# Hybrid encoder step on one core: a quarter of the first tile's expert values gathered by token during the projection and summed on VectorE

## The chip, the cores and the metric

The kernel runs on one core of a Trainium2 chip. The metric is device time in microseconds for one launch, taken as the median of several executions.

## What is computed

One layer of a streaming encoder runs over 1,024 new tokens of one stream and over 8 x 16 tokens of running streams, 9 tiles of 128 tokens in all, with rows of 1,024 float32 numbers. A token mixer (differential attention and a recurrence) comes first, behind one input projection `w_in`. Then each token picks 128 experts out of 16,384 (8 heads with 16 choices each), and the layer sums their rows:

```
eidx = jnp.take_along_axis(cidx, sel, axis=-1)
g = jax.nn.softmax(top_s, axis=-1)
act = jax.nn.gelu(jnp.einsum('td,thkd->thk', xb, u_tab[eidx]).astype(jnp.float32), approximate=False)
return jnp.einsum('thk,thkd->td', (g * act).astype(xb.dtype), v_tab[eidx])
```

So 128 tokens x 128 choices need a row of 4 KB of `u_tab` each, for a dot product with the token, and then the same number of rows of `v_tab`, weighed and summed. That is 64 MiB of each table for a tile, 1.2 GB for the nine tiles.

## The kernel before

Time is laid out in steps. Steps -330 to -1 are the head (start of the projection, mixer of the first tile). Then come eleven windows of 128 steps (`NEXP`), numbered by `i`. In window `i`, step `k` deals with choice `k` of tile `i`'s u rows and with token `k` of tile `i-1`'s v rows. Every engine's program is written out by walking these steps. Three streams of other work (`main`: the mixer of the next tile; `aside`: recurrence and running streams; `proj`: the projection) are fitted in between by their step numbers. An engine executes its own list in order, so what stands behind a waiting instruction waits too.

Window 0 holds u rows only. During it the projection of tiles 0 and 3 to 8 still runs on TensorE, and the mixer of the second tile is worked out. The v rows cannot start yet, because the ring `d_vb` that takes them holds the projection's weights and outputs until the projection ends.

The u rows are gathered by token: GpSimd issues one indirect DMA for each choice, and each of the 128 partitions receives its token's row (512 KB together). They go through a ring of `R = 4` buffers in `d_ub`. VectorE multiplies each with the normed token and adds up along the row (L1920; "dot" below), which frees the buffer. The v rows are gathered by choice: for token `k`, partition `p` receives the row of the token's choice `p` (L1726, ids turned over in `eidT`). TensorE then sums the 128 partitions with four matmuls of 256 columns (L1756), whose stationary operand is a 32-column strip of `d_dg` that ScalarE makes from the weights (L1795). The sum lands in the PSUM tile `d_pY`. VectorE adds it to the residual `d_xs`, which is read back from the scratch tensor `h` (`load_xs`, `residual`).

The weights of a tile come in two parts: `gelu` and `weigh` over choices 0 to 95 (`CUT`) near step 100, and over the last 32 at the start of the next window. The mixer's chain for a tile runs through TensorE and VectorE in turn: L911 waits for `d_oa` from VectorE (L1097), L1101 adds the output of L921 to `x`, L1105 norms it, L929 turns it, and the top-k (L1120 to L1185) gives the ids of the next window.

The gather loop of GpSimd is, for the u rows of window `i`:

```
if g >= R:
    pool.wait_ge(dot_done, g - R + 1)
off = bass.IndirectOffsetOnAxis(ap=eid[:, i % 2, k:k + 1], axis=0)
```

## Time and profile before

| | |
|---|---|
| median of 3 runs | 4042.62 us (4039.8 to 4049.7) |
| the profiled execution, its own time | 4021.32 us |
| its span, first to last instruction | 4019.0 us |
| mean granted TensorE clock | 0.748 of full speed |
| busy: PE, DVE, POOL, ACT | 2771.3, 2534.7, 2262.3, 1059.4 us |
| HBM read, written | 1352.93 MB, 33.04 MB |

PE is TensorE's matmuls, DVE VectorE, ACT ScalarE, POOL GpSimd, SP the queue that issues the plain DMAs. The 2.3 us between span and time of the profiled execution lie around the span. All figures of the rows below are of this one execution, which is 21.3 us below the median.

### The profile page before, as it was taken

To read this page: it belongs to the slowest core of one execution; us is meant where nothing else is said; L and a number is where in the kernel's file an instruction comes from. 1 tells how busy PE (TensorE), PEld (TensorE's weight loads), DVE (VectorE), ACT (ScalarE), POOL (GpSimd) and SP (SyncE) were. 2 spreads that over 40 slices of the span, in tenths; PEclk is the share of its full clock that TensorE was granted. 3 is DMA by queue.
4 is the path that set the end of the run, shared out by engine and by line. 5 is a ranking of instruction groups with operands and counts; after the bars stand their busy time and mean duration, and the time that the engine had idled before them with its cause. 6 is when DMAs were issued, how large, how long until landed. Compare 5 with 4: busy or idle time off the path is not lost.

```text
span 4019.0 us, 48466 instructions
## 1 busy us (share of the span) xinstructions
PE 2771.3 (69%) x16300; PEld 1398.7 (35%) x16300; DVE 2534.7 (63%) x6869; ACT 1059.4 (26%) x2881; POOL 2262.3 (56%) x2365
## 2 busy tenths in 40 slices
PE   6989999578568757775777487658874674333366
PEld 5845645343234324442443143315332331000011
DVE  2445657675877587758876787687677556544400
ACT  4312212332232323322332333233322111101121
POOL 1102443566666666655666666665666666666665
PEclk9989999778677867786778687868875675555567
DMA  7645798999999999999999999999999999999998
GB/s 205 192 131 167 260 335 275 343 383 377 383 374 371 393 381 375 369 383 360 379 372 382 372 370 378 390 384 347 377 381 362 376 391 352 370 375 361 366 372 315
DMA packets 545779, 1389.40 MB, mean 346 GB/s; under 512 B 61288, under 2 KB 225312, under 8 KB 545536
## 3 DMA queue, kind: packets, MB, share of 16 engines
q0 software_dynamic: 335024, 1215.35, 80.1%
q1 hardware_dynamic: 198288, 161.34, 12.6%
q10 hardware_dynamic: 12224, 9.63, 0.9%
q8 instruction: 133, 2.18, 0.2%
q14 instruction: 110, 0.90, 0.1%
HBM read 1352.93 MB, written 33.04 MB: 345 GB/s over the span
## 4 chain that ended last, share of the span: by engine, by line
PE 19%; DMA 15%; POOL 12%; DVE 10%; issue 10%; another core or an unknown queue 4%; ACT 1%; DVEq 0%; ACTq 0%; POOLq 0%
DMA d_vb<-in_peer_v_dram,d_eidT 7%; DMA d_ub<-in_peer_u_dram,d_eid 7%; PE d_pY L1756 6%; POOL d_vb L1726 6%; POOL d_ub L1707 5%; DVE d_ub L1920 4%; PE r_pB L1456 2%; PE d_pS L855 2%; PE d_pS L941 2%; PE d_pS L921 1%; PE r_pB L1471 1%; DMA d_ub<-in_peer_v_dram,d_eidT 1%; PE d_pS L880 1%; POOL d_ub L1726 1%
## 5 line engine op out<-in xcount | busy, mean ns | idle before, releaser
L1920 DVE CUSTOM_DVE_ANT_0 d_ub<-d_ub,d_pX 128x1024 f32<-128x1024 f32 x1024 | 1243.2, 1218 | 643.1 <-DMA d_ub<-in_peer_u_dram,d_eid 492.3
L1707 POOL DMA_INDIRECT d_ub<-in_peer_u_dram,d_eid x1152 | 1135.4, 986 | 890.1 <-DVE d_hdot L1920 396.5
L1756 PE MATMUL d_pY<-d_vb,d_dg 128*32 128x256 f32 x8768 | 961.4, 515 | 887.7 <-DMA d_vb<-in_peer_v_dram,d_eidT 581.4
L1726 POOL DMA_INDIRECT d_vb<-in_peer_v_dram,d_eidT x1096 | 1044.1, 953 | 722.6 <-PE d_pY L1756 262.0
L1756 PEld LDWEIGHTS d_pY<-d_vb,d_dg 128*32 128x32 f32 x8768 | 256.5, 128 | 1495.7 <-issue 1259.3
L1795 ACT ACTIVATE d_dg<-c_late_sb,d_wgtT 128x32 f32<-128x32 f32 x1152 | 335.8, 315 | 1248.6 <-PE d_pY L1756 735.3
L707 PE MATMUL d_pX<-d_wq,d_vb 128*128 128x512 f32 (+3 forms) x1536 | 470.1, 459 | 17.1 <-DMA d_vb<-in_w_in_dram 11.9
L707 PEld LDWEIGHTS d_pX<-d_wq,d_vb 128*128 128x128 f32 x1536 | 269.3, 199 | 181.7 <-issue 111.7
L1456 PE MATMUL r_pB<-r_side,c_small_sb 128*128 128x128 f32 (+15 forms) x1152 | 178.7, 325 | 19.2 <-DVE r_side L1385 10.1
L1456 PEld LDWEIGHTS r_pB<-r_side,c_small_sb 128*128 128x128 f32 x1152 | 178.2, 246 | 31.8 <-issue 17.2
L1920 DVE CUSTOM_DVE_ANT_0 d_ub<-d_ub,d_vb 128x1024 f32<-128x1024 f32 x128 | 155.6, 1225 | 48.7 <-DMA d_ub<-in_peer_u_dram,d_eid 47.9
L1888 DVE TENSOR_TENSOR d_xs<-d_xs,d_pY 128x256 f32<-128x256 f32 x36 | 15.1, 418 | 241.5 <-remote 108.4
L855 PE MATMUL d_pS<-t_shared,t_qz 128*128 128x512 f32 (+3 forms) x192 | 105.7, 684 | 20.3 <-issue 7.4
L941 PE MATMUL d_pS<-d_wq,t_AT 128*128 128x512 f32 x224 | 117.2, 651 | 1.3 <-issue 1.3
L989 ACT ACTIVATE t_AT<-d_pS 128x384 f32<-128x384 f32 (+2 forms) x120 | 50.7, 422 | 245.7 <-PE d_pS L869 134.4
L1363 DVE SCALAR_TENSOR_TENSOR r_side<-r_side,r_pB 128x128 f32<-128x128 f32 x256 | 86.8, 347 | 31.8 <-PE r_pB L1449 16.4
L562 ACT ACTIVATE d_vb<-d_pX 128x512 f32<-128x512 f32 (+2 forms) x96 | 42.8, 447 | 226.9 <-PE d_pX L707 199.9
L869 PE MATMUL d_pS<-c_small_sb,t_E 128*128 128x128 f32 x288 | 66.7, 336 | 51.6 <-issue 44.7
L1055 DVE CUSTOM_DVE_ANT_0 t_S<-d_pS,c_near 128x256 f32<-128x256 f32 (+1 forms) x128 | 51.8, 405 | 79.8 <-PE d_pS L855 56.6
L1920 DVE DVE_READ_ACCUMULATOR2_ANT d_hdot<- 128x1 f32 x1152 | 96.0, 83 | 0.0
L880 PEld LDWEIGHTS d_pS<-t_shared,t_AT 128*128 128x128 f32 x576 | 83.5, 222 | 35.7 <-issue 27.2
L855 PE MATMUL d_pS<-t_shared,d_mT 128*128 128x512 f32 (+3 forms) x192 | 92.7, 611 | 2.6 <-issue 1.0
(282 smaller groups left out, 3553.9 us busy)
## 6 DMA issues: line engine op xcount, KB each, us to landing
d_vb<-in_w_in_dram SPq DMA_DIRECT2D x68, 512.0 KB
d_ub<-in_peer_u_dram,d_eid POOLq DMA_INDIRECT x1152
d_vb<-in_peer_v_dram,d_eidT POOLq DMA_INDIRECT x1096
r_side<-in_cache_k_dram SPq DMA_DIRECT2D x16, 1024.0 KB
r_side<-in_cache_v_dram SPq DMA_DIRECT2D x16, 1024.0 KB
d_wo<-in_w_out_dram SPq DMA_DIRECT2D x6, 2048.0 KB, 9.1
d_wo<-in_peer_w_q_dram SPq DMA_DIRECT2D x4, 2048.0 KB, 8.7
scratch_h<-t_shared SPq DMA_DIRECT2D x9, 512.0 KB
```

What stands on the lines that cost most here:

```text
L707: ins = nc.tensor.matmul(pX[:, s % 2, 0:m], wring[:, n % WR, c, :], hT[:, c, a:a + m], start=c == 0, stop=c == DC - 1)
L855: ins = nc.tensor.matmul(pSf[:, at_bank[m] + a:at_bank[m] + a + n], qzs[hp % 2][:, 2 * h2 + m, :], kTf[hp % 2][:, a:a + n], start=True, st ...
L869: ins = nc.tensor.transpose(pT[:, (kb % TB) * P:(kb % TB + 1) * P], E[:, 1, kb * P:(kb + 1) * P], ident)
L880: ins = nc.tensor.matmul(pO[:, 0:VD], AT[:, kb, :], V[:, kb, h2 * VD:(h2 + 1) * VD], start=kb == 0, stop=kb == nkb - 1)
L941: m = nc.tensor.matmul(pS[:, n, :], xT[:, c, :], (wq if i >= 2 else wo)[:, c, n * 512:(n + 1) * 512], start=c == 0, stop=c == DC - 1)
L1363: nc.vector.scalar_tensor_tensor(states_[:, c, :], src, rb[:, h, last:last + 1], pB[:, 0, (c % 4) * P:(c % 4 + 1) * P], ALU.mult, ALU.add) ...
L1456: m = nc.tensor.matmul(chunks(pB[:, 1, 0:P])[:, :, j:], pick[:, SUB - 1 - j:SUB - 1 - j + P], chunks(pairs[:, j, :])[:, :, j:], start=j == ...
L1707: pool.indirect_dma_start(out=ub[:, g % R, :], out_offset=None, in_=io["peer_u"][0], in_offset=off).then_inc(u_in[g % R], 16)
L1726: pool.indirect_dma_start(out=to, out_offset=None, in_=io["peer_v"][0], in_offset=off).then_inc(landed, 16)
L1756: m = nc.tensor.matmul(pY[q * QT:(q + 1) * QT, g % 2, :], dg[:, n % DG, :], rows[:, q * QD:(q + 1) * QD], start=k % QT == 0, stop=k % QT = ...
L1795: nc.scalar.activation(dg[:, n % DG, :], hot[:, c:c + QT], ACT.Copy, scale=wgtT[:, j % 2, k:k + 1]).then_inc(dg_done, 1)
L1920: nc.vector.tensor_tensor_reduce(out=ub[:, g % R, :], in0=ub[:, g % R, :], in1=xflat if i else xn_of(0), scale=1.0, scalar=0.0, op0=ALU.mu ...
```

## The change

In window 0, the last 32 choices of the first tile (96 to 127, `OWN = 32`) get their dots first (`FIRST_ORDER`), and their weights are made at steps 36 to 38. From step 41 to step 115 their v rows are gathered too, by token, in between the u rows and through the same ring of four buffers (`own_step`, `first_rows`). For each of them VectorE does two `scalar_tensor_tensor` of 512 columns, row times weight plus running sum (`add_own`). The running sum starts as a copy of `h`; one half of it lies in PSUM in `d_pY`, the other in SBUF over `d_dg` and `wgtT` (now one tensor `d_dgw`). The last of them writes the sum back to the ring buffer, and SP stores it to the scratch tensor `h` at step 117, in place of the store of `h` in the head. In window 1 the v gathers of the first tile take 96 partitions instead of 128, and the matmuls contract 96 rows. The first tile has three gelu pieces instead of two. Two pairs of semaphores of the head are merged, which makes room for the two new ones (not shown). Everything behind window 1 is as before.

```diff
         eid, eidT = ph.sb("d_eid", [P, 2, NEXP], U32), ph.sb("d_eidT", [P, 3, P], U32)
-        gates, hdot, wgtT = ph.sb("d_gates", [P, 2, NEXP]), ph.sb("d_hdot", [P, 2, NEXP]), ph.sb("d_wgtT", [P, 2, P])
+        gates, hdot, dgw = ph.sb("d_gates", [P, 2, NEXP]), ph.sb("d_hdot", [P, 2, NEXP]), ph.sb("d_dgw", [P, DG * QT + 2 * P])
         ub, vb = ph.sb("d_ub", [P, R, D]), ph.sb("d_vb", [P, RV, D])
-        dg = ph.sb("d_dg", [P, DG, QT])
+        dg = dgw[:, 0:DG * QT].rearrange("p (n q) -> p n q", n=DG)
+        wgtT = dgw[:, DG * QT:DG * QT + 2 * P].rearrange("p (n q) -> p n q", n=2)
         qz = ph.sb("t_qz", [P, 4, P])
...
         xflat = pX[:].rearrange("p a n -> p (a n)")
+        own = [pY[:].rearrange("p a n -> p (a n)"), dgw[:, 0:512]]
 
...
             sp.wait_ge(h_done, i + 1)
-            sp.dma_start(sc["h"][t], x).then_inc(h_stored, 16)
+            if i:
+                sp.dma_start(sc["h"][t], x).then_inc(h_stored, 16)
             if i < 2:
...
                 wide_load(sp, "w_out", 1)
+            if i == 1:
+                yield own_step[-1] + 2
+                sp.wait_ge(own_done, 2 * OWN)
+                rows, _, _ = own_slot(OWN - 1)
+                sp.dma_start(sc["h"][ORDER[0]], rows).then_inc(first_stored, 16)
 
...
             nc.vector.scalar_tensor_tensor(xn_of(i), x[:], st[:, 2:3], g2[:], ALU.mult, ALU.mult).then_inc(xn_done, 1)
+            if i == 0:
+                yield local(i, R0 + 16)
+                dve.wait_ge(c_near_done, 6)
+                for n in range(2):
+                    step(nc.vector.tensor_copy(own[n], x[:, 512 * n:512 * n + 512]))
 
...
                     dve.wait_ge(r_done, 2 * i + 1)
-                    dve.wait_ge(h_stored, 16 * (i + 1))
+                    if i:
+                        dve.wait_ge(h_stored, 16 * i)
                 if g == PH:
...
         CUT = NEXP - 2 * PK
+        OWN = NEXP - CUT
+        FIRST_ORDER = list(range(CUT, NEXP)) + list(range(CUT))
+        own_step = [41 + 12 * m // 5 for m in range(OWN)]
+        first_rows = sorted([(k, 0, k) for k in range(NEXP)] + [(k, 1, m) for m, k in enumerate(own_step)])
+        at_first = {(of_v, n): a for a, (_, of_v, n) in enumerate(first_rows)}
+
+        def u_slot(g):
+            a = g + OWN if g >= NEXP else at_first[0, g]
+            return ub[:, a % R, :], u_in[a % R], 16 * (a // R + 1)
+
+        def own_slot(m):
+            a = at_first[1, m]
+            return ub[:, a % R, :], u_in[a % R], 16 * (a // R + 1)
+
+        def gelus_before(j):
+            return 2 * j + min(j, 1)
 
...
                 pool.wait_ge(c_near_psum, 4 + 2)
-                for i in range(NT + 1):
+                pool.wait_ge(ids_done, 1)
+                for a, (_, of_v, n) in enumerate(first_rows):
+                    if a >= R:
+                        _, last_v, last = first_rows[a - R]
+                        if last_v:
+                            pool.wait_ge(own_done, 2 * (last + 1))
+                            if last == OWN - 1:
+                                pool.wait_ge(first_stored, 16)
+                        else:
+                            pool.wait_ge(dot_done, last + 1)
+                    to, landed, _ = own_slot(n) if of_v else u_slot(n)
+                    k = CUT + n if of_v else FIRST_ORDER[n]
+                    pool.indirect_dma_start(out=to, out_offset=None, in_=io["peer_v" if of_v else "peer_u"][0],
+                                            in_offset=bass.IndirectOffsetOnAxis(ap=eid[:, 0, k:k + 1], axis=0)).then_inc(landed, 16)
+                for i in range(1, NT + 1):
                     for k in range(NEXP):
...
                                 pool.wait_ge(ids_done, 2 * i + 1)
-                            if g >= R:
-                                pool.wait_ge(dot_done, g - R + 1)
+                            pool.wait_ge(dot_done, g - R + 1)
+                            to, landed, _ = u_slot(g)
                             off = bass.IndirectOffsetOnAxis(ap=eid[:, i % 2, k:k + 1], axis=0)
-                            pool.indirect_dma_start(out=ub[:, g % R, :], out_offset=None, in_=io["peer_u"][0],
-                                                    in_offset=off).then_inc(u_in[g % R], 16)
+                            pool.indirect_dma_start(out=to, out_offset=None, in_=io["peer_u"][0], in_offset=off).then_inc(landed, 16)
                         if i:
...
                                 pool.wait_ge(exp_used, n - (RV + R if n >= LAST + RV + R else RV) + 1)
-                            off = bass.IndirectOffsetOnAxis(ap=eidT[:, (i - 1) % 3, k:k + 1], axis=0)
+                            some = CUT if i == 1 else P
+                            off = bass.IndirectOffsetOnAxis(ap=eidT[0:some, (i - 1) % 3, k:k + 1], axis=0)
                             to, landed, _ = v_slot(n)
-                            pool.indirect_dma_start(out=to, out_offset=None, in_=io["peer_v"][0], in_offset=off).then_inc(landed, 16)
+                            pool.indirect_dma_start(out=to[0:some], out_offset=None, in_=io["peer_v"][0],
+                                                    in_offset=off).then_inc(landed, 16)
                 for n in range(R):
-                    pool.wait_ge(u_in[n], 16 * (NT * NEXP // R))
+                    pool.wait_ge(u_in[n], 16 * ((NT * NEXP + OWN) // R))
                 for n in range(RV + R):
...
                 def turn_weights(j):
-                    pe.wait_ge(wgt_done, 2 * (j + 1))
+                    pe.wait_ge(wgt_done, gelus_before(j + 1))
                     if j + 1 < NT:
...
                     g = k // QT
+                    some = P if j else CUT
                     if k % QT == 0 and 4 * j + g:
                         pe.wait_ge(h2_done, 4 * j + g)
+                    if n == 0:
+                        pe.wait_ge(own_done, 2 * OWN)
                     for q in range(4):
-                        m = nc.tensor.matmul(pY[q * QT:(q + 1) * QT, g % 2, :], dg[:, n % DG, :],
-                                             rows[:, q * QD:(q + 1) * QD], start=k % QT == 0, stop=k % QT == QT - 1)
+                        m = nc.tensor.matmul(pY[q * QT:(q + 1) * QT, g % 2, :], dg[0:some, n % DG, :],
+                                             rows[0:some, q * QD:(q + 1) * QD], start=k % QT == 0, stop=k % QT == QT - 1)
                     m.then_inc(exp_used, 1)
...
                 def gelu(j, a, b):
-                    act.wait_ge(dot_done, NEXP * j + b)
+                    act.wait_ge(dot_done, NEXP * j + (b if j else (b + OWN) % NEXP or NEXP))
                     nc.scalar.activation(hdot[:, j % 2, a:b], hdot[:, j % 2, a:b], ACT.Gelu).then_inc(gelu_done, 1)
...
                         rows_written(act, NSEG - 1)
-                    act.wait_ge(h_stored, 16 * (j + 1))
+                    if j:
+                        act.wait_ge(h_stored, 16 * j)
+                    else:
+                        act.wait_ge(first_stored, 16)
                     of = sc["h"][ORDER[j]].rearrange("(g j) (q c) -> q j g c", g=4, q=4)
...
                         proj.until(NEXP * i + k)
+                        if i == 0 and k == OWN + 4:
+                            gelu(0, CUT, NEXP)
                         if i < NT and k == CUT + 4:
-                            gelu(i, 0, CUT)
+                            gelu(i, 0, CUT if i else CUT - OWN)
                         if i == 1 and k == 0:
...
                             if k == 0:
-                                gelu(j, CUT, NEXP)
+                                gelu(j, *((CUT, NEXP) if j else (CUT - OWN, CUT)))
                                 if i < NT:
...
                                 act.wait_ge(wT_psum, j + 1)
+                                if j == 0:
+                                    act.wait_ge(own_done, 2 * OWN)
                                 nc.scalar.activation(wgtT[:, j % 2, :], pT[:, 0:P], ACT.Copy).then_inc(wT_done, 1)
...
                 def weigh(j, n, a, b):
-                    dve.wait_ge(gelu_done, 2 * j + n + 1)
+                    dve.wait_ge(gelu_done, gelus_before(j) + n + 1)
                     nc.vector.tensor_tensor(hdot[:, j % 2, a:b], hdot[:, j % 2, a:b], gates[:, j % 2, a:b],
                                             ALU.mult).then_inc(wgt_done, 1)
+
+                def add_own(m):
+                    rows, landed, count = own_slot(m)
+                    dve.wait_ge(landed, count)
+                    if m:
+                        dve.wait_ge(own_done, 2 * m)
+                    for n in range(2):
+                        half = rows[:, 512 * n:512 * n + 512]
+                        ins = nc.vector.scalar_tensor_tensor(own[n] if m < OWN - 1 else half, half, hdot[:, 0, CUT + m:CUT + m + 1], own[n],
+                                                             ALU.mult, ALU.add)
+                        ins.then_inc(own_done, 1)
 
...
                     if i <= NT:
-                        weigh(i - 1, 1, CUT, NEXP)
+                        weigh(i - 1, *((1, CUT, NEXP) if i > 1 else (2, CUT - OWN, CUT)))
                     if i >= 2:
...
                             g = NEXP * i + k
-                            dve.wait_ge(u_in[g % R], 16 * (g // R + 1))
+                            rows, landed, count = u_slot(g)
+                            dve.wait_ge(landed, count)
                             if i and k == 0:
                                 dve.wait_ge(x_copied, i)
-                            nc.vector.tensor_tensor_reduce(out=ub[:, g % R, :], in0=ub[:, g % R, :], in1=xflat if i else xn_of(0), scale=1.0,
+                            c = k if i else FIRST_ORDER[k]
+                            nc.vector.tensor_tensor_reduce(out=rows, in0=rows, in1=xflat if i else xn_of(0), scale=1.0,
                                                            scalar=0.0, op0=ALU.mult, op1=ALU.add,
-                                                           accum_out=hdot[:, i % 2, k:k + 1]).then_inc(dot_done, 1)
+                                                           accum_out=hdot[:, i % 2, c:c + 1]).then_inc(dot_done, 1)
+                        if i == 0 and k == OWN + 6:
+                            weigh(0, 0, CUT, NEXP)
+                            dve.wait_ge(wgt_done, 1)
+                        if i == 0 and k in own_step:
+                            add_own(own_step.index(k))
                         main.until(NEXP * i + k)
...
                         if i < NT and k == CUT + 6:
-                            weigh(i, 0, 0, CUT)
+                            weigh(i, *((0, 0, CUT) if i else (1, 0, CUT - OWN)))
                         if i >= 2:
```

On VectorE, in window 0 around step 41, this stood before (L1920 is the dot, `d_vb` holds the first tile's normed tokens):

```order
L1920 ISA d_ub,d_hdot<-d_ub,d_vb 128x1024 [waits d_u_in1]
L1920 ISA d_hdot 128x1
L1920 ISA d_ub,d_hdot<-d_ub,d_vb 128x1024 [waits d_u_in2]
L1920 ISA d_hdot 128x1
L1055 ISA t_S,t_tiny<-d_pS,c_near 128x256 [waits t_s_psum]
L1055 ISA t_tiny 128x1
L1066 TENSOR_SCALAR t_tiny<-t_tiny 128x1 [waits t_near_max]
```

And now there stands, with the dot at L1987 and the additions at L1946:

```order
L1987 ISA d_ub,d_hdot<-d_ub,d_vb 128x1024 [waits d_u_in1]
L1987 ISA d_hdot 128x1
L1946 SCALAR_TENSOR_TENSOR d_pY<-d_ub,d_hdot,d_pY 128x512 [waits d_u_in2]
L1946 SCALAR_TENSOR_TENSOR d_dgw<-d_ub,d_hdot,d_dgw 128x512
L1987 ISA d_ub,d_hdot<-d_ub,d_vb 128x1024 [waits d_u_in3]
L1987 ISA d_hdot 128x1
L1062 ISA t_S,t_tiny<-d_pS,c_near 128x256 [waits t_s_psum]
L1062 ISA t_tiny 128x1
L1073 TENSOR_SCALAR t_tiny<-t_tiny 128x1 [waits t_near_max]
```

A pair of additions, with a wait for a landing of its own, has come in behind a dot, and the next dot uses the buffer after it. This happens 32 times.

On GpSimd, the gathers of window 0 and the first of window 1 were before:

```order
L1707 DMA d_ub<-in_peer_u_dram,d_eid 128x1024 [waits d_dot_done] x124
L1707 DMA d_ub<-in_peer_u_dram,d_eid 128x1024 [waits d_dot_done,d_ids_done]
L1726 DMA d_vb<-in_peer_v_dram,d_eidT 128x1024 [waits p_zT_out0,p_turned,p_zT_out1,p_acc,d_ids_done]
L1707 DMA d_ub<-in_peer_u_dram,d_eid 128x1024 [waits d_dot_done]
L1726 DMA d_vb<-in_peer_v_dram,d_eidT 128x1024
```

Now they are, from the last two v rows by token on:

```order
L1739 DMA d_ub<-in_peer_v_dram,d_eid 128x1024 [waits d_dot_done]
L1739 DMA d_ub<-in_peer_u_dram,d_eid 128x1024 [waits d_own_done]
L1739 DMA d_ub<-in_peer_u_dram,d_eid 128x1024 [waits d_dot_done] x2
L1739 DMA d_ub<-in_peer_u_dram,d_eid 128x1024 [waits d_first_stored,d_own_done]
L1739 DMA d_ub<-in_peer_u_dram,d_eid 128x1024 [waits d_dot_done] x8
L1750 DMA d_ub<-in_peer_u_dram,d_eid 128x1024 [waits d_dot_done,d_ids_done]
L1769 DMA d_vb<-in_peer_v_dram,d_eidT 96x1024 [waits p_zT_out0,p_turned,p_zT_out1,p_acc,d_ids_done]
```

One u gather (of step 119) now waits for SP's store of the sum, and the v gathers of window 1 have 96 rows.

On SP, the loads of the recurrence (L1238 to L1240) were followed at once by the projection's last stores (L479, L481). Now the store of the sum (L843) stands between them and waits for VectorE's last addition, so the projection's last stores are queued behind that wait.

## Rows read from the trace of the kernel before

**Rows 1.** The page: span, busy time, and the DMA engines in 40 slices.
```profile
span 4019.0 us, 48466 instructions
...
PE 2771.3 (69%) x16300; PEld 1398.7 (35%) x16300; DVE 2534.7 (63%) x6869; ACT 1059.4 (26%) x2881; POOL 2262.3 (56%) x2365
...
DMA  7645798999999999999999999999999999999998
```

**Rows 2.** Busy time by stretch: start:end, length, engines, granted clock, DMA share, GB/s.
```profile
362.00:476.00 114.00, 114.00 (x457) 70.27 (x457) 83.21 (x205) 32.62 (x87) 43.70 (x39) 0.98 0.72 236
476.00:534.00 58.00, 51.88 (x147) 26.92 (x146) 37.84 (x73) 8.04 (x18) 31.69 (x28) 0.94 0.94 319
534.00:599.00 65.00, 62.51 (x183) 31.70 (x183) 29.41 (x54) 9.07 (x14) 24.64 (x22) 1.00 0.98 360
599.00:650.00 51.00, 49.73 (x157) 26.22 (x156) 36.54 (x154) 9.39 (x16) 16.53 (x16) 1.00 0.82 265
650.00:690.00 40.00, 40.00 (x122) 21.01 (x121) 37.96 (x132) 6.87 (x13) 16.87 (x17) 1.00 0.89 288
690.00:730.00 40.00, 20.03 (x67) 10.83 (x65) 19.81 (x41) 16.74 (x29) 13.65 (x13) 0.80 0.73 253
730.00:1123.00 393.00, 272.48 (x1661) 131.75 (x1661) 283.33 (x801) 113.66 (x318) 246.35 (x257) 0.73 1.00 379
1123.00:1506.00 383.00, 271.37 (x1682) 135.73 (x1682) 285.12 (x807) 113.13 (x322) 242.51 (x254) 0.73 1.01 380
1000.00:1050.00 50.00, 30.75 (x212) 14.79 (x208) 44.88 (x184) 13.25 (x32) 31.03 (x34) 0.64 1.01 385
1050.00:1100.00 50.00, 27.45 (x180) 11.32 (x180) 42.48 (x149) 16.24 (x33) 33.09 (x34) 0.64 1.02 394
```

**Rows 3.** The page, DMA queues: packets, MB, share of 16 engines' span.
```profile
q0 software_dynamic: 335024, 1215.35, 80.1%
```

**Rows 4.** What VectorE waited for, 476 to 690 us: total, times, longest.
```profile
DVE d_ub L1920 <- DMA d_ub<-in_peer_u_dram,d_eid: 40.5, 38, 4.2
DVE d_hdot L1882 <- ACT d_hdot L1788: 12.7, 1, 12.7
DVE t_shared L1120 <- ACT t_E L1038: 10.3, 1, 10.3
DVE t_shared L1101 <- PE d_pS L921: 7.8, 1, 7.8
```

**Rows 5.** What TensorE waited for, 476 to 690 us: total, times, longest.
```profile
PE d_pS L911 <- DVE d_oa L1097: 6.1, 1, 6.1
PE d_pS L929 <- DVE d_xn L1105: 2.5, 1, 2.5
```

**Rows 6.** VectorE in order of time: start, duration, instruction, idle before it.
```profile
557.60 1.22 DVE L1920 CUSTOM_DVE_ANT_0 d_ub<-d_ub,d_vb 128x1024 f32<-128x1024 f32 x1 [0.30 <-DMA d_ub<-in_peer_u_dram,d_eid]
...
559.20 1.22 DVE L1920 CUSTOM_DVE_ANT_0 d_ub<-d_ub,d_vb 128x1024 f32<-128x1024 f32 x1 [0.37 <-DMA d_ub<-in_peer_u_dram,d_eid]
...
561.77 1.23 DVE L1920 CUSTOM_DVE_ANT_0 d_ub<-d_ub,d_vb 128x1024 f32<-128x1024 f32 x1 [1.35 <-DMA d_ub<-in_peer_u_dram,d_eid]
```

**Rows 7.** VectorE instruction groups by shape: count, busy, mean ns.
```profile
L1436 DVE SCALAR_TENSOR_TENSOR d_mixT<-r_side,c_hgn 128x512 f32<-128x512 f32 x9 | 6.8, 752 | 0.3
...
L1888 DVE TENSOR_TENSOR d_xs<-d_xs,d_pY 128x256 f32<-128x256 f32 x36 | 15.1, 418 | 241.5 <-remote 108.4 <-PE d_pY L1756 95.3 <-issue 37.6
...
L1105 DVE SCALAR_TENSOR_TENSOR d_xn<-t_shared,d_st,c_g 128x1024 f32<-128x1024 f32 x8 | 10.3, 1285 | 0.3
```

**Rows 8.** The page, costliest groups: the two gathers as GpSimd issues them.
```profile
L1707 POOL DMA_INDIRECT d_ub<-in_peer_u_dram,d_eid x1152 | 1135.4, 986 | 890.1 <-DVE d_hdot L1920 396.5
...
L1726 POOL DMA_INDIRECT d_vb<-in_peer_v_dram,d_eidT x1096 | 1044.1, 953 | 722.6 <-PE d_pY L1756 262.0
```

**Rows 9.** VectorE in order of time at the end of the projection.
```profile
688.28 1.22 DVE L1920 CUSTOM_DVE_ANT_0 d_ub<-d_ub,d_vb 128x1024 f32<-128x1024 f32 x1
...
705.10 1.12 DVE L1325 TENSOR_SCALAR r_side<-r_side,c_lbt 128x128 f32<-128x128 f32 x4 [13.66 <-ACT r_side L1280]
```

13 lines of the change are left out of this document (6 added, 7 removed).

## The prediction, made before the changed kernel ran

> **What bounds the kernel now.** I read the page first, for its line of DMA shares over the span [rows 1]: from the ninth slice on (about 800 us) it reads 9 nearly throughout, that is 90% or more, while no engine is busy for more than 69% of the span. The stretches say it more exactly [rows 2]: window 1 (730 to 1123 us) and window 2 (1123 to 1506 us) have DMA shares of 1.00 and 1.01. From there on the kernel is as long as its transfers. Window 0 (362 to 730 us) is different. The DMA engines are 72% busy up to 476 us (step 41), then 94, 98, 82 and 89% up to 690 us, and 73% in the last 40 us. TensorE is busy there: all of 114 us, 51.88 of 58, 62.51 of 65, 49.73 of 51, 40 of 40. So window 0 is TensorE's, with the projection, and the DMA engines have little left in it.
>
> The waits tell how tightly VectorE hangs on both sides there [rows 4]. In 476 to 690 us it waits 40.5 us, in 38 pieces, for u rows to land, and three times for the mixer: 7.8 us for L921, 10.3 for L1120's scores, 12.7 for the gelu. And in two places TensorE already waits for VectorE [rows 5]: 6.1 us at L911, and 2.5 at L929.
>
> **The change, part by part.** Bytes are moved and none are saved, so the first question is what a gather costs in DMA time. The software queue takes 80.1% of 16 engines' 4019.0 us for 1215.35 MB [rows 1, 3], 3219 us. The 2304 gathers of 0.524 MB are 1208 MB of it, so one takes 3219 x 1208 / 1215.35 / 2304 = 1.389 us of all 16 engines. The 32 rows by token are 44.4 us. The 128 gathers of window 1 that lose a quarter of their rows lose 128 x 0.25 x 1.389 = 44.4 us too.
>
> *Window 0, the DMA side.* What the DMA engines have free between 476 and 730 us is the sum of length times idle share [rows 2]: 58 x 0.06 + 65 x 0.02 + 51 x 0.18 + 40 x 0.11 + 40 x 0.27 = 3.5 + 1.3 + 9.2 + 4.4 + 10.8 = 29.2 us. The free 28% before 476 us (32 us) stay free, since the first row by token is gathered near step 41. The 10.8 us at the end lie behind the last of them (step 115, near 678 us) and around the change of windows; I count a third of them. So 18.4 + 3.6 = 22.0 of the 44.4 us fit in, and window 0 grows by 22.4 us. Ends: all 29.2 us are used, growth 15.2; nothing is used, growth 44.4.
>
> *Window 0, the VectorE side,* as a cross-check. Of a `scalar_tensor_tensor` with 512 columns in SBUF the trace has one at 752 ns, one of 1,024 columns at 1285 ns, and a sum out of PSUM over 256 columns at 418 ns [rows 7]. I take 0.70 us, so 1.4 us for a row and 45 us for all 32 (ends 1.28 and 1.5 us a row, 41 and 48 us). VectorE also needs more landings from the same four buffers: where it runs behind nothing but landings, dots are 1.6 to 2.6 us apart, with waits of 0.30 to 1.35 us each [rows 6], so a further row costs 1.4 to 2.1 us there. Up to L1097 (near 510 us; seven rows by token, of steps 41 to 55, stand ahead of it) TensorE is the one that waits already [rows 5], so 7 x 1.4 to 2.1 = 10 to 15 us pass straight on to it. From there to the L921 wait there are four rows, 6 to 8 us, with 7.8 us of cover. Between the waits of 7.8 and 10.3 us lie nine rows, 13 to 19 us against 10.3: 3 to 9 us late. The next seven rows, 10 us, hide in the wait of 12.7. The last five, 7 us, hide in the 13.66 us that VectorE waits for the recurrence's ACT at 691 us [rows 9]. Together 13 to 24 us, which agrees with 22.4 from the DMA side. I keep 22.4.
>
> *The store.* SP's store of the sum waits for the last addition, and the u gather of step 119 waits for the store. Before, that dot ran at 688.28 and VectorE then waited until 705.10 [rows 9]. A store issued behind L1240's load lands when this wait is nearly over, so I give it nothing beyond its bytes: 0.524 MB, as much as a gather, now in busy time: +1.4 us. If it comes late, the projection's last stores on SP, queued behind it, come late as well, and with them the first v gathers; that is up to 10 us. The copy of `h` on VectorE (two of 512 columns, nearest row 752 ns, so 1.5 us) lies in the head behind the norm that TensorE waits for; the third gelu and its multiply are two small instructions beside VectorE's waits. These count nothing; uncovered they would be 1.5 and about 3 us.
>
> *Window 1.* All 44.4 us come off if the DMA engines stay as full as they are. Two engines stand in the way. VectorE is busy for 283.33 of 393 us, but for 44.88 and 42.48 of 50 us in 1000 to 1100 us [rows 2]. That stretch would shrink by 100 x 44.4 / 393 = 11.3 to 88.7 us with 87.4 us of VectorE's work in it, which would leave it 1.3 us for waits in place of 12.6. I let it keep 6 to 7, so 5 us are not gained. GpSimd issues two gathers a step, 986 and 953 ns [rows 8], 246.35 us in the window [rows 2]; they were 63% of it and would be 71%, with the v gathers perhaps shorter for their 96 rows and perhaps not (bounds 0.715 and 0.953 us). For the waits between them I take off another 3 us. That leaves 44.4 - 8 = 36.4 us; ends 44.4 and, if a gather of 96 rows lasts as long as one of 128, 0. TensorE (272.48 of 393 us) has room.
>
> No row shows a gather of fewer than 128 rows, so its transfer may take anything from three quarters of 1.389 us (1.04, rows dealt evenly over the engines) to 1.389 (some engines keep all of theirs). I take 1.04. The Trainium skill bears on this in two places, and no run here has shown either. "DMA: Bandwidth & Descriptors", section "Why a DMA increments its semaphore by 16 and not by 1", says that the number of engines is the largest up to 16 that divides the partition count, and gives 96 partitions as a case of 16. By that rule the saving is the full 44.4 us. The section "The descriptor swizzle" of the same page ties each engine of a 128-partition transfer to its own partitions, engines 0 to 7 to partitions 0 to 63 and the others to the rest. If that held for 96 too, eight engines would keep all eight rows and only the other eight would lose theirs, and the sum would lose its 44.4 us.
>
> **The sum.** +22.4 (window 0) + 1.4 (store) - 36.4 (window 1) = -12.6 us. Windows 2 to 9 are left as they are. Against the profiled execution (4021.3 us, span 4019.0) that is 4008.7, and against the median 4042.6 - 12.6 = 4030.0 us.
>
> **Rivals.** A difference under 0.3% (12.1 us) is about what a measurement of this kernel cannot tell from none, and the forecast lies on that edge.
>
> A. As summed: about half of the moved work fills idle DMA time and most of the saving arrives. 4020 to 4040 us. Chance 0.50.
>
> B. Window 1 does not get shorter because a 96-row gather holds the busiest DMA engines as long as before. For it: no row shows a smaller gather, so nothing excludes the upper bound of 1.389 us. Against it: the gathers make up nearly all of a full DMA share, and rows that are not asked for must leave time free on at least some engines. Then 4042.6 + 22.4 + 1.4 - (0 to 10) = 4056 to 4066 us, slower. It decides as soon as less than 24 of the 44.4 us arrive. Chance 0.12. The swizzle in the Trainium skill, cited above, would be the mechanism of this rival, and the skill's rule on 96 partitions speaks against it.
>
> C. Window 0 grows by all of the added work. The ring is shared by 1.4 rows a step, VectorE falls behind, and TensorE, which waits for it already [rows 5], stops at L911, L929 and the top-k. For it: 40.5 us of landing waits with the ring as it is [rows 4]. Against it: three waits with 30.8 us of cover. Growth 34 to 44 us: 4042 to 4053 us, no change or slower. Chance 0.16.
>
> D. The idle time is used better: VectorE keeps up, window 0 grows by 10 to 15 us and window 1 loses its 40 to 44. 4042.6 + 12.5 + 1.4 - 42 = 4014 us, between 4010 and 4020. Chance 0.22.
>
> **How the numbers follow.** The predicted time is A's, 4030. 4010 to 4053 leaves out B (0.12) and some of the edges. Faster by over 0.3% means below 4030.5: half of A (0.25) and nearly all of D (0.21), 0.46. Slower means above 4054.7: B and the end of C, 0.18. The rest, 0.36, is within 0.3%.
>
> **What would show it.** In the profile after: the first dot of window 1 (L1987 on `d_pX`) about 22 us later than at 730 us; DMA share 0.97 or more from 476 to 690 us; L1946 at about 0.7 us each; TensorE's wait at L911 grown from 6.1 to 16 us or more; window 1 about 357 us long (393 before), with a DMA share of 0.96 to 1.0 and VectorE near its limit towards the window's end; windows from 2 on unchanged within some us. If window 1 stays above 380 us at a full DMA share, B is right. If window 0 grows by over 34 us, C. I would be wrong in another way if the v gathers of window 1 started late because the last stores of the projection wait behind the sum on SP.

## The result, and the profile after

| | before | after |
|---|---|---|
| median (6 runs each) | 4042.33 us (4034.35 to 4049.7) | 4181.18 us (4174.83 to 4223.54) |
| the profiled execution, its span | 4021.32, 4019.0 us | 4190.81, 4188.7 us |
| ratio, 95% interval | | 1.035 (1.0325 to 1.0375) |

The changed kernel is slower by 3.5%, 139 us. The forecast was 4030 with a range of 4010 to 4053: the sign is wrong, and no rival reached so far. The two profiled executions lie 169.5 us apart, since the one of before was 21 us under its median and the one of after 10 us over it; some 30 us of what follows belong to that.

First, the page of the changed kernel, its span, its DMA line with the GB/s below it, and the software queue (before: [rows 1, 3]).

```profile
span 4188.7 us, 48602 instructions
...
DMA  7635799999999999999999999999999999999998
GB/s 204 185 120 182 264 357 324 286 263 256 254 243 358 369 385 375 363 378 380 358 371 381 378 365 363 390 373 376 368 377 358 374 393 354 366 369 367 359 364 317
...
q0 software_dynamic: 335536, 1215.36, 81.1%
```

The queue moves the same bytes (1215.36 MB), as it should. The DMA line alone hides the fault: it reads 9 from the sixth slice on, much as before. The line below it tells. From the eighth to the twelfth slice (733 to 1257 us) the same full engines move 243 to 286 GB/s, afterwards 354 to 393 until the last slice.

The window table of the changed kernel answers to [rows 2] (start:end, length, busy time of PE, PEld, DVE, ACT, POOL with counts, granted clock, DMA share, GB/s). Window 0 now runs from 366 to 763 us, window 1 from 763 to 1273.

```profile
366.00:476.00 110.00, 110.00 (x447) 68.51 (x446) 79.41 (x193) 31.66 (x85) 42.27 (x37) 0.98 0.73 239
476.00:534.00 58.00, 43.63 (x122) 22.86 (x121) 42.09 (x84) 10.15 (x23) 31.66 (x27) 0.88 0.89 294
534.00:599.00 65.00, 52.51 (x133) 25.74 (x132) 39.69 (x61) 4.57 (x9) 35.20 (x31) 0.89 0.97 352
599.00:650.00 51.00, 51.00 (x165) 27.24 (x164) 37.47 (x104) 8.68 (x13) 22.47 (x23) 1.00 1.01 362
650.00:690.00 40.00, 40.00 (x123) 20.87 (x122) 34.92 (x122) 8.27 (x15) 17.61 (x19) 1.00 1.02 348
690.00:730.00 40.00, 39.06 (x120) 20.47 (x119) 34.98 (x118) 8.42 (x16) 14.28 (x13) 1.00 0.95 322
730.00:763.00 33.00, 7.31 (x27) 4.06 (x25) 21.64 (x43) 12.93 (x22) 17.47 (x17) 0.63 0.89 315
763.00:1273.00 510.00, 296.15 (x1661) 140.06 (x1660) 285.30 (x801) 114.75 (x317) 242.77 (x256) 0.64 1.04 257
1273.00:1665.00 392.00, 274.46 (x1683) 134.92 (x1683) 285.66 (x806) 113.15 (x322) 244.93 (x256) 0.72 1.00 375
```

Where the 169.7 us of span went: 4.4 in the head, 28.4 in window 0 (368.7 to 397.0 us, from first dot to first dot), 117.4 in window 1 (392.5 to 509.9), 9.1 in window 2, and some 10 spread over the rest. Window 1 is the result. It moves fewer bytes than before, with DMA engines that are busy all the time (1.04), at 257 GB/s in place of 379. Such a row gives the time of a 4 KB row of a table on its engine: 16 engines x share x 4096 B / rate. That was 16 x 1.00 x 4096 / 379 = 173 ns, and is 16 x 1.04 x 4096 / 257 = 265 ns. In window 2, where every gather has 128 rows again, it is 175 ns. Below, "row time" is this number. It is a mean; the trace also has the time of each row's packet by itself. In window 1 before, three quarters of the rows took 165 ns or less; now nine in ten take 216 ns or more. The rows fetched with 128 partitions must be among them, since they are more than half of all.

What waited in window 1 of the changed kernel, 780 to 1270 us (total, times, longest):

```profile
POOL d_ub L1750 <- DVE d_hdot L1987: 209.4, 117, 3.6
DVE d_ub L1987 <- DMA d_ub<-in_peer_u_dram,d_eid: 193.4, 97, 4.6
PE d_pY L1803 <- DMA d_vb<-in_peer_v_dram,d_eidT: 188.4, 85, 4.4
```

Both consumers wait for landings, VectorE for the u rows too, which the change did not touch. GpSimd waits for dots: the ring is full, so it is not the issue of gathers that is short.

What TensorE waited for at the end of window 0 of the changed kernel, 476 to 760 us (before: [rows 5], and the last line here, of 690 to 730 us before; L918, L936 and L971 are L911, L929 and L964 of before):

```profile
PE d_pS L936 <- DVE d_xn L1112: 12.5, 1, 12.5
PE d_pS L918 <- DVE d_oa L1104: 10.6, 1, 10.6
PE d_pS L971 <- DVE t_shared L1198: 8.9, 1, 8.9
...
PE d_pS L964 <- DVE t_shared L1185: 2.8, 1, 2.8
```

The store of the sum shows too. GpSimd waits 10.5 us for it ahead of the gather of step 119, and VectorE then waits 6.37 us for that gather's row. Before, VectorE waited 13.66 us for ScalarE at the next step ([rows 9]; L1280 there is L1293 here). Now ScalarE is done at 731.90 us (731.27 + 0.63), and VectorE gets to that step only at 738.17, without a wait:

```profile
POOL d_ub L1739 <- DMA scratch_h<-d_ub: 10.5, 1, 10.5
...
735.08 1.23 DVE L1987 CUSTOM_DVE_ANT_0 d_ub<-d_ub,d_vb 128x1024 f32<-128x1024 f32 x1 [6.37 <-DMA d_ub<-in_peer_u_dram,d_eid]
...
731.27 0.63 ACT L1293 ACTIVATE r_side<-r_side 128x512 f32<-128x512 f32 x1
```

Without its wait VectorE would have been there at 731.80 (738.17 - 6.37), when ScalarE was ready. From this point to the first dot of window 1 it takes 25.2 us, and took 25.5 before, so up to some 6 us of window 0's growth can be the wait for the store. The v gathers of window 1 don't start late: the first is issued at 754.0 us, 1.2 us behind the first u gather of the window.

And the additions, in the changed kernel's groups by shape:

```profile
L1946 DVE SCALAR_TENSOR_TENSOR d_pY<-d_ub,d_hdot,d_pY 128x512 f32<-128x512 f32 x31 | 23.4, 755 | 21.9 <-DMA d_ub<-in_peer_v_dram,d_eid 21.8
L1946 DVE SCALAR_TENSOR_TENSOR d_dgw<-d_ub,d_hdot,d_dgw 128x512 f32<-128x512 f32 x31 | 23.1, 746 | 0.0
```

### The profile page after: what moved, and what is told of

Read it like the earlier page. It is cut to its first block, busy times and chain, and to the rows that moved or that the text cites. A ratio compares the mean times of both kernels' runs of the same rounds, so it can differ in the third digit from the quotient of the medians.

```text
span 4188.7 us, 48602 instructions
## 1 busy us (share of the span) xinstructions
PE 2820.1 (67%) x16300; PEld 1422.7 (34%) x16300; DVE 2584.0 (62%) x6936; ACT 1060.1 (25%) x2883; POOL 2293.1 (55%) x2397
## 3 DMA queue, kind: packets, MB, share of 16 engines
q0 software_dynamic: 335536, 1215.36, 81.1%
## 4 chain that ended last, share of the span: by engine, by line
DMA 23%; PE 18%; POOL 12%; DVE 12%; issue 9%; another core or an unknown queue 5%; ACT 1%; DVEq 0%; ACTq 0%; POOLq 0%
DMA d_ub<-in_peer_u_dram,d_eid 15%; DMA d_vb<-in_peer_v_dram,d_eidT 8%; POOL d_vb L1769 6%; PE d_pY L1803 6%; POOL d_ub L1750 6%; DVE d_ub L1987 5%; PE r_pB L1469 3%; PE d_pS L862 2%; PE d_pS L948 2%; PE d_pS L928 1%; PE d_pS L887 1%; PE d_pS L966 1%; POOL d_ub L1769 1%; PE d_pS L876 1%
## 5 line engine op out<-in xcount | busy, mean ns | idle before, releaser
L1987 DVE CUSTOM_DVE_ANT_0 d_ub<-d_ub,d_pX 128x1024 f32<-128x1024 f32 x1024 | 1243.2, 1218 | 780.2 <-DMA d_ub<-in_peer_u_dram,d_eid 669.9
L1803 PE MATMUL d_pY<-d_vb,d_dgw 128*32 128x256 f32 (+1 forms) x8768 | 966.9, 522 | 998.4 <-DMA d_vb<-in_peer_v_dram,d_eidT 754.1
L1803 PEld LDWEIGHTS d_pY<-d_vb,d_dgw 128*32 128x32 f32 (+1 forms) x8768 | 256.3, 128 | 1612.3 <-issue 1401.7
L1842 ACT ACTIVATE d_dgw<-c_late_sb,d_dgw 128x32 f32<-128x32 f32 x1152 | 335.4, 315 | 1287.5 <-PE d_pY L1803 810.8
L1987 DVE CUSTOM_DVE_ANT_0 d_ub<-d_ub,d_vb 128x1024 f32<-128x1024 f32 x128 | 155.7, 1222 | 54.0 <-DMA d_ub<-in_peer_u_dram,d_eid 52.6
L887 PE MATMUL d_pS<-t_shared,t_AT 128*128 128x64 f32 x576 | 97.5, 327 | 10.4 <-issue 6.5
L862 PE MATMUL d_pS<-t_shared,d_mT 128*128 128x512 f32 (+3 forms) x192 | 101.8, 663 | 2.0 <-ACT t_E L988 1.5
```

Source lines behind the costliest of these rows:

```text
L862: ins = nc.tensor.matmul(pSf[:, at_bank[m] + a:at_bank[m] + a + n], qzs[hp % 2][:, 2 * h2 + m, :], kTf[hp % 2][:, a:a + n], start=True, st ...
L887: ins = nc.tensor.matmul(pO[:, 0:VD], AT[:, kb, :], V[:, kb, h2 * VD:(h2 + 1) * VD], start=kb == 0, stop=kb == nkb - 1)
L1803: m = nc.tensor.matmul(pY[q * QT:(q + 1) * QT, g % 2, :], dg[0:some, n % DG, :], rows[0:some, q * QD:(q + 1) * QD], start=k % QT == 0, sto ...
L1842: nc.scalar.activation(dg[:, n % DG, :], hot[:, c:c + QT], ACT.Copy, scale=wgtT[:, j % 2, k:k + 1]).then_inc(dg_done, 1)
L1987: nc.vector.tensor_tensor_reduce(out=rows, in0=rows, in1=xflat if i else xn_of(0), scale=1.0, scalar=0.0, op0=ALU.mult, op1=ALU.add, accum ...
```

## The experiments

The runs came from four chips. The kernel before took 3835.18 us on that of a_v128, b_v96, b_v96_all and b_v64, 4048.3 on that of b_v64_alt, b_v64_s2, b_v112 and a_noadd, 3832.71 on that of a_packed and b_shapes, and 3834.94 on that of a_packed_late. Each ratio is against the kernel before on the same chip, and window lengths are compared on one chip or between the three quick ones. The theory was that the 96-row gather is what costs, the rivals that something else which the change brings does: the additions, the order of SP's store, or VectorE's time.

**a_v128: the changed kernel with full v gathers.** The gathers of window 1 fetch 128 rows again; the matmuls still sum 96. So all the work that the change adds is there, and none that it saves.

```
-                            some = CUT if i == 1 else P
+                            some = P
```

> The changed kernel with one part undone: in window 1 the v gathers take 128 rows again, of which TensorE still contracts 96; everything in window 0 is as in the change. Theory P (a gather of 96 rows slows all row transfers that are in flight with it): window 1 falls from 510 to about 393 us and the mean 4 KB row from 257 to about 170 ns, and the kernel takes what window 0 costs alone, about 4042 + 33 = 4075 us. Rival Q (something that the change brings to window 1 with it, such as the sum in d_pY and d_dgw or the shifted ring of d_ub, is what slows it): window 1 stays near 510 us and the time near 4180.

3859.26 us, ratio 1.0069 (1.0043 to 1.0095). Windows of this run around window 0's end and window 1 (758 to 1134):

```profile
476.00:534.00 58.00, 44.41 (x117) 22.95 (x116) 41.30 (x75) 7.60 (x17) 34.14 (x30) 0.85 0.91 310
534.00:599.00 65.00, 57.04 (x143) 27.56 (x142) 37.82 (x59) 6.16 (x10) 29.64 (x28) 0.92 1.02 373
...
690.00:730.00 40.00, 35.09 (x109) 18.25 (x107) 32.76 (x106) 11.41 (x18) 15.15 (x16) 1.00 0.94 320
730.00:758.00 28.00, 2.04 (x6) 1.08 (x6) 21.32 (x44) 8.88 (x18) 15.05 (x13) 0.51 0.98 372
758.00:1134.00 376.00, 274.00 (x1660) 136.09 (x1660) 284.63 (x802) 113.44 (x320) 247.78 (x256) 0.69 1.01 387
```

Window 1 is an ordinary one again (376 us, 387 GB/s), although it moves more bytes. Window 0 keeps its growth (396.3 us, against 364.5 to 367.4 in b_v64, b_v96 and b_v96_all on this chip). The 0.69% are 26.5 us (16 to 36 by the interval): the added work alone, against the forecast's 23.8. As store and additions are all there too, neither can be what lengthens window 1.

**b_v96: the kernel before with 96-row gathers in window 1.** Only gather and matmul of window 1 are cut to 96 partitions; the last 32 choices of the first tile are left out of the sum. **b_v96_all** does so for every tile (`if True`), and leaves out the last 32 choices of all.

```
+                            some = 96 if (i - 1) == 0 else P
+                            off = bass.IndirectOffsetOnAxis(ap=eidT[0:some, (i - 1) % 3, k:k + 1], axis=0)
-                            pool.indirect_dma_start(out=to, ...
+                            pool.indirect_dma_start(out=to[0:some], ...
```

> The kernel before with one part of the change alone: the v gathers of the first tile (window 1) take rows 0 to 95 and TensorE contracts 96. It leaves out the last 32 choices of the first tile from the sum. Theory P: window 1 takes about 510 us as in the changed kernel, though 16.8 MB fewer are moved, and the kernel about 4042 + 117 = 4160 us. Rival Q: window 1 is shorter than 393 us, about 350 to 365, and the kernel about 4010 us.

> The kernel before with the v gathers of all nine tiles at 96 rows (leaves out the last 32 choices of every tile). The last window has v gathers alone, 193 us for 128 of them before, 1.51 us each. If 96-row gathers are slow by themselves, this window takes longer than 193 us although it moves a quarter less; if they only disturb the u gathers of 128 rows beside them, it takes about 160 us (1.25 us each, GpSimd's own pace of issuing). The eight windows with both kinds take about 510 us each by theory P, so the kernel about 362 + 369 + 8 x 510 + 150 to 220 = 4960 to 5030 us; by rival Q about 3750.

b_v96: 3990.87 us, ratio 1.0403 (1.0381 to 1.0424), although nothing is added and 16.8 MB less are moved. Its windows 0 and 1:

```profile
362.00:730.00 368.00, 338.78 (x1126) 187.37 (x1124) 245.25 (x657) 84.39 (x181) 148.52 (x132) 0.96 0.84 285
730.00:1258.00 528.00, 306.94 (x1660) 146.41 (x1660) 284.43 (x800) 112.77 (x311) 243.34 (x256) 0.62 1.03 248
```

b_v96_all: 4917.39 us, ratio 1.2818 (1.2775 to 1.2861), with windows 1 to 7 of 489 to 520 us. The last 128 gathers run without u gathers beside them. From the issue of the first to that of the last they take 201.5 us here, 1.57 us each, and 168.6 us in a_v128, 1.32 us each for 128 rows. From those stretches (4703 to 4905 us, and 3667 to 3836 in a_v128), first of b_v96_all:

```profile
4700.00:4900.00 200.00, 132.12 (x979) 29.12 (x979) 9.02 (x20) 42.80 (x137) 114.88 (x127) 0.50 1.02 254
```

and of a_v128:

```profile
3660.00:3820.00 160.00, 103.33 (x919) 24.84 (x915) 11.10 (x22) 39.61 (x127) 112.50 (x121) 0.69 1.02 400
```

So the cost is in the gather itself, in every window. There are two parts. Alone, 96 rows take 1.57 us where 128 take 1.32. Beside u gathers it gets worse: a pair takes 528 / 128 = 4.13 us, and the two apart would be 1.32 + 1.57 = 2.89.

**b_v64, b_v112: other counts.** The same edit with 64 and 112 (they leave out 64 and 16 choices of the first tile).

> The kernel before with the v gathers of the first tile (window 1) at 64 rows, 0 to 63 (leaves out half of the first tile's choices). If what slows the transfers is that the number is no power of two or no full set, 64 rows, a power of two, go at the usual 159 to 170 ns a row and window 1 falls to about 393 - 89 = 305 to 330 us. If it is which rows an engine gets and to which partitions they go (64 rows dealt four to an engine, so that two engines write into partitions that one served before), rows are slow again, above 220 ns, and window 1 stays above 400 us.

> The kernel before with v gathers of 112 rows in window 1 (leaves out 16 choices of the first tile). 8 times 2048 rows fewer than before. If the slowdown grows with how few rows a gather has, window 1 is near 393 us; if any number but 128 brings it (P2), rows take 250 ns or more and window 1 about 540 us (15 rows an engine and step at 0.26 us and 0.3 to 0.4 us of other transfers), longer than with 96 rows (510 to 529) or 64 (467).

b_v64: 3917.44 us, ratio 1.0211 (1.0188 to 1.0235), window 1 467 us. b_v112: 4207.31 us, ratio 1.0405 (1.0357 to 1.0453), window 1 549 us. The rows of window 1, of b_v64:

```profile
725.60:1192.90 467.30, 304.80 (x1660) 145.81 (x1660) 285.10 (x802) 114.07 (x317) 240.99 (x256) 0.62 1.02 243
```

and of b_v112:

```profile
724.00:1273.00 549.00, 305.02 (x1644) 145.62 (x1644) 284.11 (x796) 115.71 (x317) 247.13 (x257) 0.62 1.04 255
```

The row time is 275 and 267 ns, much as with 96 rows. The length then follows the number of rows: the loss is not an effect of 96.

**b_v64_alt, b_v64_s2: the same 64 rows in other partitions.** Window 1's gathers from the sixth on fetch 64 rows, either five gathers into partitions 0 to 63 and five into 64 to 127 in turn, or all into every second partition (`to[0:P:2]` in place of the line below). Half of the first tile's v rows are left out.

```
+                            if i == 1 and k >= RV:
+                                to = to[64:P] if k // RV % 2 else to[0:64]
```

> The kernel before with 64-row v gathers in window 1 (from the sixth on) whose rows land in partitions 0 to 63 five times and then in 64 to 127 five times; the rows fetched are those of choices 0 to 63 throughout and the sum takes whatever lies in the buffers, so the first tile's output is not the reference's. Theory P1 (slow because half of the partitions take the load: u rows everywhere, v rows in one half): the load is even over some steps, and window 1 falls from 467 to some 300 to 340 us with rows under 200 ns. Theory P2 (slow whenever a gather has other than 128 rows, because its rows are then dealt so that two DMA engines write into partitions that one serves in a gather of 128): stays at 440 to 470 us, rows at 260 to 275 ns.

> The kernel before with 64-row v gathers in window 1 (from the sixth on) whose rows land in every second partition, 0, 2, ... 126 (choices 0 to 63 are fetched, the sum takes whatever lies in the buffers, so the first tile's output is not the reference's). Here all partition groups take the same load, and each DMA engine's four rows go to eight neighbouring partitions. P1 (load on one half): window 1 at 300 to 330 us, rows near 170 ns. P2 in the form 'any other number than 128 is slow': as with 64 rows in partitions 0 to 63, 467 us and 270 ns. P2 in the form 'engines that meet in a partition group': in between, 340 to 440 us, 190 to 250 ns, since at most two engines meet in a group.

b_v64_alt: 4095.02 us, ratio 1.0127 (1.0074 to 1.0181), window 1 455 us with a row time of 267 ns. As up to nine gathers are under way at once (the rings have four and five buffers), five of one kind in a row are no strong test of whether the two halves balance. b_v64_s2: 4046.18 us, ratio 1.0004 (0.9982 to 1.0025). Its windows 1 and 2:

```profile
724.00:1115.00 391.00, 271.72 (x1660) 134.02 (x1660) 282.55 (x800) 111.75 (x315) 240.64 (x255) 0.73 0.88 295
1115.00:1507.00 392.00, 277.14 (x1682) 139.02 (x1682) 286.87 (x807) 113.16 (x323) 244.34 (x255) 0.73 1.00 373
```

The same 64 rows, spread over all 128 partitions, have a row time of 195 ns in place of 267 in b_v64_alt on this chip (275 in b_v64), and leave the engines idle for 12%. The pattern of partitions decides, not the count. Yet the window is as long as the next one, so something other than transfers set its length. Of the three expectations, those with rows near 170 and at 270 ns did not come; the one in between did.

**b_shapes: another shape in each window.** The kernel before, with the v gathers of the eight full windows at 16, 32 and 64 rows from partition 0, 64 rows on every second and 32 on every fourth partition, 96 rows from partition 32, 80 and 120 rows from partition 0; and at the end, without u gathers, 32 each of 128, 64, 64 on every second, and 112 rows. It leaves out the v rows that these gathers don't fetch, and was timed once: 4307.45 us.

```
+        SHAPES = [(0, 16, 1), (0, 32, 1), (0, 64, 1), (0, 64, 2), (0, 32, 4), (32, 96, 1), (0, 80, 1), (0, 120, 1)]
+        TAIL = [(0, 128, 1), (0, 64, 1), (0, 64, 2), (0, 112, 1)]
```

> The kernel before with another shape of v gather in each window (the sums take whatever lies in the buffers, so the outputs are not the reference's): window 1: 16 rows from partition 0; window 2: 32 rows; 3: 64 rows; 4: 64 rows on every second partition; 5: 32 rows on every fourth; 6: 96 rows from partition 32; 7: 80 rows; 8: 120 rows; the last window, v gathers alone, in four parts of 32: 128, 64, 64 on every second partition, 112 rows. Theory M (a gather of fewer rows into consecutive partitions is dealt so that DMA engines write into partition groups that another serves, and they hold one another up): rows of 4 KB take 240 to 280 ns on average in windows 3, 6, 7, 8, less in 1 and 2 (few v rows), and near 165 to 190 in 4 and 5. Theory N (slow when few engines take all of the rows): the engines' share falls below 0.9 in the slow windows. And on what holds a window when transfers do not: if it is transfers alone, windows 1 and 5 fall to 230 to 280 us; if the engines' own chain holds it near 390 us, they stay above 340.

Its windows in that order, and then the four pieces without u gathers:

```profile
725.70:1074.00 348.30, 245.45 (x1660) 126.51 (x1660) 280.95 (x802) 112.73 (x322) 236.06 (x254) 0.77 0.83 259
1074.00:1430.20 356.20, 252.86 (x1682) 128.25 (x1682) 284.30 (x807) 112.94 (x325) 239.54 (x259) 0.76 0.94 272
1430.20:1902.60 472.40, 303.57 (x1742) 153.49 (x1742) 295.01 (x814) 119.41 (x328) 244.71 (x256) 0.67 1.03 242
1902.60:2251.20 348.60, 253.40 (x1702) 129.85 (x1702) 287.31 (x787) 116.97 (x323) 240.25 (x257) 0.77 0.91 319
2251.20:2589.70 338.50, 254.53 (x1726) 127.92 (x1726) 291.85 (x794) 121.35 (x336) 240.19 (x257) 0.80 0.85 283
2589.70:3113.60 523.90, 324.61 (x1814) 160.00 (x1814) 304.88 (x821) 127.61 (x337) 245.54 (x257) 0.68 1.04 251
3113.60:3572.30 458.70, 224.46 (x1366) 97.39 (x1366) 238.30 (x593) 72.09 (x199) 243.27 (x257) 0.61 1.01 253
3572.30:4103.10 530.80, 134.65 (x994) 29.17 (x994) 155.33 (x257) 45.25 (x141) 240.18 (x249) 0.50 1.03 241
4103.10:4152.00 48.90, 27.22 (x227) 7.14 (x227) 7.38 (x15) 12.82 (x44) 30.04 (x32) 0.60 0.95 328
4152.00:4196.60 44.60, 28.30 (x260) 7.13 (x264) 0.42 (x1) 10.34 (x33) 28.59 (x33) 0.69 1.04 241
4196.60:4235.70 39.10, 26.44 (x296) 7.84 (x295) 0.42 (x1) 11.96 (x38) 28.38 (x32) 0.85 0.83 233
4235.70:4281.40 45.70, 27.42 (x216) 6.02 (x216) 0.42 (x1) 8.56 (x27) 28.44 (x31) 0.57 1.00 272
```

With u gathers beside them, every run of 64 and more consecutive partitions that isn't all 128 is slow, wherever it starts: row times of 279 (64), 272 (96 from 32), 262 (80) and 280 ns (120), windows of 459 to 531 us. Every second and every fourth partition are quick (187 and 197 ns), in windows of 349 and 339 us. 16 and 32 rows lie between (210 and 226 ns), too few to cost much. The slow windows have DMA shares of 1.01 to 1.04, so theory N, that few engines take all of the rows, does not hold.

The quick windows do not fall below 339 us. In the one of 338.5 us (32 rows on every fourth partition) GpSimd is busy for 240.19 us, and between two of its 256 gathers nearly always lie 0.30 us, which makes 240 + 77 = 317 us: its own pace of issuing is nearly as long as the window. VectorE has 291.85 us of work there.

The four pieces without u gathers are short, and each begins with gathers of the piece before still in flight, so their lengths (1.53, 1.39, 1.22 and 1.47 us from one issue to the next) are no clean prices. On every second partition 1.22 us is GpSimd's own pace (0.89 us and a gap of 0.30 for each), with 17% of DMA time idle. For 64 rows from partition 0 and for 112 rows the stretches in the middle say more, 4160 to 4190 and 4245 to 4275 us:

```profile
4160.00:4190.00 30.00, 19.01 (x179) 4.84 (x176) 0.42 (x1) 7.39 (x23) 19.65 (x22) 0.71 1.04 213
4245.00:4275.00 30.00, 19.17 (x144) 3.90 (x136) 0.00 (x0) 5.75 (x18) 18.58 (x22) 0.50 1.03 277
```

A gather's bytes over the rate give its time: 0.262 MB / 213 = 1.23 us for 64 rows, 0.459 MB / 277 = 1.66 for 112, and in the same way 1.55 for 96 (254 GB/s, b_v96_all) and 1.31 for 128 (400 GB/s, a_v128). Half the rows thus save next to nothing, and 96 or 112 take longer than 128. A row of the 64 takes 320 ns, twice the 16 x 1.02 x 4096 / 400 = 167 ns of the full gather.

**a_noadd: the additions cut.** a_v128 with the 64 additions on 8 columns in place of 512 (the first tile's last 32 choices are mostly left out).

```
-                        half = rows[:, 512 * n:512 * n + 512]
+                        half = rows[:, 512 * n:512 * n + 8]
```

> The changed kernel with 128-row v gathers in window 1 (as in a_v128), and with VectorE's 64 additions of window 0 cut from 512 to 8 columns: gathers, waits and order are all there, about 64 x 0.55 = 35 us of VectorE's work are not. The sum of the first tile is not the reference's. If window 0 grows because of the transfers and the shared ring (my prediction's reckoning by DMA time), it stays about 20 to 29 us longer than before, and the kernel 0.5 to 0.7% slower; if it is VectorE's time, window 0 is within 8 us of before and the kernel within 0.2%.

4077.31 us, ratio 1.0070 (1.0047 to 1.0093), the same as a_v128's 1.0069. Window 0 takes 391.1 us, 23 to 28 more than in b_v112, b_v64_alt and b_v64_s2 on this chip, whose window 0 is that of before (368.2, 368.4, 363.5). With the additions it was 28 in the changed kernel and 29 to 32 in a_v128. So most of the growth is not VectorE's 48 us of additions (64 of 0.75). How much of it is theirs the runs do not tell closely: the windows alone allow 1 to 9 us, and VectorE's wait for the row behind the store is 8.40 us here, against 3.71 in a_v128 and 6.37 in the changed kernel, so the store can stand for a part that the additions had there.

**a_packed: the saving as whole gathers.** The changed kernel, but window 1's 96 rows a token are packed: three gathers of 128 rows serve four tokens (96 of one token, and in partitions 96 to 127 a third of the fourth token's). 96 gathers and 96 groups of matmuls are left of 128. Nothing is left out.

```
+        def v_number(j, k):
+            return NEXP * j + k - 32 if j else k - k // 4
...
+                    if j == 0 and k % 4 == 3:
+                        return
...
+                        nc.scalar.activation(dg[0:96, n % DG, :], hot[0:96, c:c + QT], ACT.Copy, scale=wgtT[0:96, 0, k:k + 1])
+                        nc.scalar.activation(dg[96:128, n % DG, :], hot[96:128, c3:c3 + QT], ACT.Copy,
```

> The changed kernel with the same saving in full gathers: in window 1 three gathers of 128 rows serve four tokens (rows 0 to 95 of each for one token, rows 96 to 127 for a third of the fourth token's 96 choices), so 96 gathers, 96 x 4 matmuls and 96 issues of GpSimd in place of 128. Nothing is left out of the computation. If only the shape of the gather spoiled the saving and window 1 is as long as its transfers, window 1 falls by 35 to 44 us from some 390 (rows near 170 ns), and with 26 to 29 us more in window 0 the kernel is 8 to 16 us faster than before (ratio 0.996 to 0.998). If window 1 is held by more than its transfers (in b_v64_s2 it kept 391.6 us at a DMA share of 0.88 with half of its v rows gone), it falls by less than 20 us, and the kernel is 5 to 25 us slower than before (ratio 1.001 to 1.006).

3832.99 us, ratio 1.0001 (0.9988 to 1.0014). Window 0 takes 396.0 us, window 1 345.4, at the full rate:

```profile
757.00:1102.00 345.00, 238.04 (x1400) 124.45 (x1396) 281.95 (x801) 139.22 (x385) 216.24 (x225) 0.71 1.00 374
```

That is 30 us under a_v128's 375.4 on another chip (26 by the two ratios). It pays back the 31 us of window 0 (365.0 in b_shapes on this chip) and no more. Neither expectation came: window 1 fell by less than 35 us and by more than 20, and the kernel is neither faster nor slower.

**a_packed_late: the rows by token later.** a_packed, with `own_step` written out from step 58 to 115, so that fewer of them stand ahead of L1104.

```
-        own_step = [41 + 12 * m // 5 for m in range(OWN)]
+        own_step = [58, 59, 61, 62, 64, 71, 74, 77, 79, 82, 84, 86, 88, 89, 91, 92, 94, 96, 98, 100, 101,
+                    103, 104, 105, 106, 107, 109, 110, 112, 113, 114, 115]
```

> a_packed with the 32 rows by token at other steps of window 0: none before step 58 (before it, TensorE waits for VectorE at the product with d_oa, 6.1 us in the kernel before and 9.7 in a_packed) and none in steps 65 to 70 (the norm of the second tile, for which TensorE waited 2.5 us before and 11.5 in a_packed); the 32 lie in steps 58 to 64 and 71 to 115, where VectorE had waits of 7.8, 10.3, 12.7 and 13.7 us to cover them. If it is these two waits through which the added rows lengthen window 0, both are back within 2 us of the kernel before, window 0 grows by 12 to 18 us in place of 28, and the kernel is 8 to 16 us faster than before (ratio 0.996 to 0.998). If window 0 grows by what the DMA engines cannot take in, wherever the rows stand, it stays 24 to 30 us longer, the waits move to the later places where TensorE takes VectorE's results, and the ratio stays at 1.000.

3832.87 us, ratio 0.9998 (0.9983 to 1.0013); window 0 395.8 us, window 1 341.6. TensorE's waits in a_packed (476 to 756 us; L921, L939, L974 are L911, L929, L964 of before):

```profile
PE d_pS L939 <- DVE d_xn L1115: 11.5, 1, 11.5
...
PE d_pS L921 <- DVE d_oa L1107: 9.7, 1, 9.7
PE d_pS L974 <- DVE t_shared L1201: 9.1, 1, 9.1
```

and in a_packed_late:

```profile
PE d_pS L974 <- DVE t_shared L1201: 23.6, 1, 23.6
...
PE d_pS L939 <- DVE d_xn L1115: 5.9, 1, 5.9
...
PE d_pS L921 <- DVE d_oa L1107: 3.5, 1, 3.5
```

30.3 us of waits became 33.0: they moved to the last place of the chain, and window 0 and the ratio stayed, as the second half of the expectation has it. The growth of window 0 does not depend on which wait shows it.

## Why the prediction was wrong

**The step that failed** is "No row shows a gather of fewer than 128 rows, so its transfer may take anything from three quarters of 1.389 us ... to 1.389". It was taken as 1.04. That was too low, the upper end too, and the larger fault is that the price was sought in the gather alone. Window 1 took 117.4 us more in place of 36.4 less, an error of 154 us; the miss as a whole is 151. Measured: 1.57 us for 96 rows alone against 1.32 for 128, and 4.13 us for a pair with a u gather against 2.93 (a_v128's 376 / 128). Nearly every row of the window slowed down, from 173 to 265 ns in the mean.

**Rival B** named the place and the sign, with a chance of 0.12, and its sign, window 1 above 380 us at a full DMA share, is what the profile shows (510 us at 1.04). But it stopped at 1.389 us, that is at no gain; a smaller gather that slows the others was in no rival. The range fell short for that reason.

**Window 0, DMA side** (+22.4, and +1.4 for the store): +28.4 us in the profile, 26.5 us by a_v128's ratio. That the moved rows cost more than idle time can take in holds, since the growth stays with the additions gone (a_noadd) and with other waits (a_packed_late). No run separates the DMA engines' time from waits for landings in the shared ring of four buffers. The share in 476 to 690 us was forecast at 0.97 or more and was 0.89, 0.97, 1.01 and 1.02: the first stretch, at 0.94 before, did not fill but fell, and kept 58 x 0.11 = 6.4 us idle. C, with 34 us or more, did not come.

**The store** was given nothing beyond its bytes, since it would land when a wait of VectorE is nearly over. That wait of 13.66 us is gone in the changed kernel, and VectorE waits 6.37 us for the row behind the store. This and the unfilled first stretch are each large enough for the 4.6 us by which the two terms (23.8) fall short of 28.4; no run moves the store, so their parts are not shown.

**Window 0, VectorE side.** 0.70 us an addition was 0.75. The wait at L911 was forecast at 16 us or more and is 10.6; more stands at L929 (12.5, was 2.5) and L964 (8.9, was 2.8). The three grew by 20.6 us together, within the 13 to 24 of the forecast, but not where it had them. That both sides of the forecast agreed on 22 us was no proof of VectorE's price: the growth is nearly the same without its additions.

**Window 1's other terms.** With full gathers the saving of 36.4 us is 26 to 30 (a_packed). Its window still has a DMA share of 1.00, and GpSimd's issues with their gaps make only 216 + 225 x 0.30 = 284 of its 345 us, so there the transfers are still the limit. In b_shapes' windows with fewer rows GpSimd's pace comes close, 317 of 339 us (its chain was not followed further). So the sum with its mechanism mended is +31 - 30, no change, as a_packed shows. No version ran faster than the kernel before.

**The chances.** The 0.18 for slower counts "the end of C", but C as written ends at 4053 us, below the 4054.7 at which slower begins; only B's 0.12 had a range there.

**What makes the gather slow** is partly argued. Shown: which partitions the rows go to decides, and with half the rows, in partitions 0 to 63 alone, each row takes twice the time (320 ns against 167) at a DMA share of 1.04. Another pattern may also deal the rows to the engines in another way, and the trace does not tell which engine moved a row. The numbers fit rows dealt evenly to 16 engines which then meet at the entrances of half the partitions, but that is argued, not shown. The Trainium skill, "SBUF — State Buffer", section "Door 1: The DMA port swizzle (why `[64,N]` ≈ `[32,N]`)", has 16 ports of eight partitions each, where partitions 0 to 63 reach only eight. Worked out from that table (an estimate), the fullest port of a gather has eight rows for 128, 112, 96 and 64 consecutive partitions, and four for 64 rows on every second. That agrees with 64 consecutive rows being as slow a gather as 128 (1.23 and 1.31 us) and with the quick rows on every second partition (187 ns against 279). It does not account for 112 and 96 rows, which take 1.66 and 1.55 us with the same eight rows on the fullest port. The Trainium skill's rule cited in the prediction, 16 engines for 96 partitions, agrees with the full DMA share (1.04), but the saving that I drew from it does not follow: a row takes longer on its engine. The Trainium skill's section "The descriptor swizzle", cited as B's mechanism, would leave eight engines with fewer rows than the others, hence a share under 1, and the trace does not show that.

**What stays open.** Why a short gather and a full one together take so much more than the two apart (4.13 against 2.89 us). Why 120 and 112 rows, beside u gathers, are as slow a row as 64. How window 0's growth divides between transfers, the shared ring, the store and VectorE. And why b_v64_s2, with 12% idle DMA time on its slower chip, kept a window of 391 us.

## What to carry to other kernels

A gather's price was not its bytes here: before one is made smaller, look at which partitions its rows reach, and keep it at all 128 or spread it over all of them (64 rows on every second and 32 on every fourth partition were quick); save whole gathers, by packing. Look at the other engines' pace too: GpSimd's issues with their gaps filled 317 us of a window of 339, with 32 rows in each v gather. A full DMA share says that engines are occupied, not how fast they move data (1.00 went with 379 GB/s and 1.04 with 257), so read GB/s beside it. When work is moved from a full stretch into another, price the resource that both share: here window 0 grew by 28 us for 44 us of moved transfers. And a cover that a term relies on can be gone in the changed kernel, as the wait of 13.66 us was that should have covered the store.

## What the runs showed of the hardware

- Mean row time (4 KB) of a window with gathers into n consecutive partitions beside full ones: 173 ns (128, before), 280 (120), 267 (112, b_v112), 272 (96 from 32), 262 (80), 275 (64, b_v64), 226 (32), 210 (16); on every second partition 187 (64), on every fourth 197 (32), where no run is named from b_shapes.
- A gather without u gathers beside it, by bytes and rate: 1.31 us (128, a_v128), 1.66 (112, b_shapes), 1.55 (96, b_v96_all), 1.23 (64, b_shapes).
- GpSimd issues a 96-row gather in 0.91 us (changed kernel, window 1), a 128-row one in 0.94 (window 2), with 0.30 us or more between two. The rows hardly matter there.
- Chips of one kind differ: the same kernel took 4048 us on one and 3833 to 3835 on three others, over 5% apart, more than most edits to it are worth.
